# The second half of a decoder's key tiles in products of 256 columns, and its activations 96 bytes further on

## The chip, the core and the metric

The kernel runs on one core of one Trainium2 chip, one program launched once. The time is the device time in microseconds (us), the median of the runs of a kernel. Engines are called as in the profile: PE is the matrix engine TensorE and PEld its weight loads, ACT is ScalarE, DVE is VectorE, POOL is GpSimd, SP issues the loads from memory.

## The reference

One block of a decoder over 256 tokens of width 1024: first a mixer of a convolution branch and a dilated attention branch, then a retrieval from 16384 experts. The retrieval is what the change touches:

```
q = (xc @ w_q).reshape(TOKEN_CHUNK, PEER_HEADS, 2, half)
s = jnp.einsum('thpd,hpnd->thpn', q, sub_keys)
top_s, top_i = lax.top_k(s, PEER_TOPK)
...
e = i1 * PEER_N_KEYS + i2
gate = jax.nn.softmax(best_s, axis=-1)
h = jnp.einsum('thkd,td->thk', u_tab[e], xc)
act = jax.nn.gelu(h, approximate=False) * gate
return jnp.einsum('thk,thkd->td', act, v_tab[e])
```

## The kernel before

The kernel does not gather experts. It computes the product of every expert row of `u_tab` with every token, takes the gelu, multiplies by a gate that is zero for experts a token has not picked, and multiplies the result by all of `v_tab`. Each table is read as 128 tiles of 128 x 1024 numbers. The program has a front part (76 weight tiles and the attention), then 128 key tiles (U) and then 128 value tiles (V).

**Precision.** Every tile comes in float32 into `raw`. ACT rounds it into `hi` (line 335) and DVE or POOL writes the rest `raw - hi` into `lo` (line 354). The other operand is split the same way: the normed tokens into `nrm_hi` and `nrm_lo`, the activations into `act_hi` and `act_lo`. A product of two numbers is then hi times hi, hi times lo and lo times hi.

**Key tiles 0 to 63** run in `u_tile`: per tile 8 blocks of 128 numbers, and per block three products of 256 columns into one bank: 24 products a tile (line 1242, in `product`). `hi` or `lo` is the operand that PE loads as weights (stationary), the tokens stream through (moving). ACT then takes the gelu out of the bank (line 645).

**Key tiles 64 to 127** run in `wide_tile`. `nrm_hi` and `nrm_lo` of a block lie side by side, so `hi` meets both in one product of 512 columns (line 1499), whose right half goes into the right half of the bank; `lo` meets `nrm_hi` in one of 256 (line 1501). That is 16 products a tile. The two halves of the bank have to be added: ACT copies the right one into `half_sum` (line 666), DVE adds the left one (line 1167), and ACT takes the gelu of the sum (line 671). PE may write a bank again when `added` says that the tile two before has been summed.

**The gates.** Beside these tiles run 32 groups of small products (line 1513, 16 to a group, 128 x 64 in float16) that spread the gates of 8 tokens over the experts of the first half. DVE makes their operands and multiplies the gates into `act`. The first two groups stand ahead of tiles 64 and 66, the others in pairs ahead of every fourth tile. PE thus starts a row of large products 17 times. Another 32 groups stand among the first 64 value tiles in the same way.

**Value tiles** run in `v_tile`: 12 products of 512 columns each (line 1564, the last two tiles in line 1590), and here `act_hi` and `act_lo` are the weights and `hi` and `lo` stream. The activations lie in the space of the tokens, which are no longer needed: the two views of `norm_space` are

```
norm_space = sb("norm_space", [P, KB * 2 * T + SHIFT], F32R)
nrm = norm_space[:, SHIFT:].rearrange("p (k a t) -> p k a t", a=2, t=T)
picked_acts = norm_space[:, 0:RING * 2 * T].rearrange("p (k a t) -> p k a t", a=2, t=T)
```

Every slice that PE loads or streams starts at a multiple of 512 bytes from the start of its view. So all slices of a view have one place modulo 512. Counted from the start of `norm_space`, the tokens are at place 32, the activations at 0, and `hi` and `lo` at 96. `rounded_space`, which holds the streamed operand in parts of the front, is placed at 32 as well.

**The order of the work** is written out by hand, with semaphores between engines. `raw`, `hi` and `lo` have 4 slots each; SP loads a tile into a slot when its `lo` is done.

Of the kernel before, what the change touches and what calls it, by code (L numbers as in the profile page):

```python
# [11 lines left out]
ALU = mybir.AluOpType  # L12
ACT = mybir.ActivationFunctionType
AX = mybir.AxisListType

P = 128
D = 1024
T = 256
KB = D // P
# [23 lines left out]
RING = 4  # L43
LEAD = 3
AHEAD = 2

SHIFT = 8
CHUNK_STEPS = PH // 2 + 9
TOP_TILES = 48
EXP_TILE = 52  # L50
PICK_TILE = 60
HALF = NK // 2
# [112 lines left out]
def hybrid_block(nc, x_t, front, cols, rel_bias, onehot, sub_keys, u_tiles, v_tiles, out):  # L165
    bias_row = nc.dram_tensor("bias_row", (HEADS, BW), F32, kind="Internal").ap()
    toeplitz = nc.dram_tensor("toeplitz", (HEADS, P * BW), F32, kind="Internal").ap()
    with ExitStack() as ctx:
        def sb(name, shape, dt=F32, stack=ctx):
            return stack.enter_context(nc.sbuf_tensor(name, shape, dt))  # L170

        def sem(name):
            return ctx.enter_context(nc.semaphore(name))

        bank = [ctx.enter_context(nc.psum_tensor(f"bank{i}", [P, 512], F32)) for i in range(8)]


        norm_space = sb("norm_space", [P, KB * 2 * T + SHIFT], F32R)
        nrm = norm_space[:, SHIFT:].rearrange("p (k a t) -> p k a t", a=2, t=T)
        nrm_hi, nrm_lo = nrm[:, :, 0, :], nrm[:, :, 1, :]  # L180
        picked_acts = norm_space[:, 0:RING * 2 * T].rearrange("p (k a t) -> p k a t", a=2, t=T)
        act_hi, act_lo = picked_acts[:, :, 0, :], picked_acts[:, :, 1, :]
        ident = sb("ident", [P, P])
        iota = sb("iota", [P, TOPK])
# [35 lines left out]
        act = sb("act", [P, NK, T])  # L220
# [3 lines left out]
        parts = sb("parts", [P, T // PAIR, 2, PAIR], F16)  # L224
        ohA = sb("ohA", [P, 2, TOK // PAIR, NK, PAIR], F16)
        eqB = sb("eqB", [P, TOK // PAIR, HALF, PAIR], F16)
        half_sum = sb("half_sum", [P, 2, T])
        ohB = sb("ohB", [P, 2, TOK // PAIR, 2, HALF, PAIR], F16)
        raw = sb("raw", [P, RING, D])
        hi = sb("hi", [P, RING, D], F32R)  # L230
        lo = sb("lo", [P, RING, D], F32R)
# [42 lines left out]
        pe_step = sem("pe_step")  # L274
# [15 lines left out]
        attn_gated, merged, m_hi = sem("attn_gated"), sem("merged"), sem("m_hi")  # L290
        chain = sem("chain")
        sc_ready = sem("sc_ready")
        crossed, added, gelu_done = sem("crossed"), sem("added"), sem("gelu_done")
        top_done, gexp, gate_ready, pick_T, pick_ready = [sem(s) for s in (
            "top_done", "gexp", "gate_ready", "pick_T", "pick_ready")]
        second, spread, gate_mm, gated = sem("second"), sem("spread"), sem("gate_mm"), sem("gated")
        blocks_free = sem("blocks_free")
# [31 lines left out]
        def split_hi(act_e, base, it, j):  # L329

            s = slot_of(base, j)
            wait_raw(act_e, base, it, j)
            if not (isinstance(it, int) and base + 4 * it + j < RING):
                wait(act_e, pe_step, step_of(base - 4, it, j))
            act_e.copy(hi[:, s, :], raw[:, s, :]).then_inc(hi_ready, 1)  # L335
# [11 lines left out]
        def wait_lo(eng, base, it, j):  # L347
            eng.wait_ge(lo_ready[slot_of(base, j)], uses(base, it, j))
# [116 lines left out]
        def _(a):  # L465
# [193 lines left out]
                    gelu(0, it, j)  # L659

            a.wait_ge(pick_ready, 2)
            def copy_cross(it, j):

                a.wait_ge(pe_step, it * 4 + (S_U + HALF + j + 1))
                a.wait_ge(gelu_done, it * 4 + (HALF + j - 1))
                a.copy(half_sum[:, j % 2, :], bank[4 + j % 2][:, T:2 * T]).then_inc(crossed, 1)  # L666

            def gelu_sum(base, it, j):

                a.wait_ge(added, it * 4 + (base + j + 1))  # L670
                a.activation(act[:, it * 4 + (HALF + base + j), :], half_sum[:, (base + j) % 2, :], ACT.Gelu)\
                 .then_inc(gelu_done, 1)

            def a_split(base_i, it, j):

                wait(a, pe_step, it * 4 + (S_V + base_i + j - 3))
                a.copy(act_hi[:, (base_i + j) % RING, :], act[:, it * 4 + (base_i + j), :]).then_inc(a_hi, 1)  # L677

            def key_round(it, first=False, last=False):
                for j in range(RING):  # L680
                    if last and j == RING - 1:
                        a.wait_ge(gated, GROUPS_N)
                        a.wait_ge(blocks_free, 1)
                        for first_act in range(AHEAD):
                            a_split(first_act, 0, 0)
                    copy_cross(it, j)
                    if not (first and j == 0):
                        gelu_sum(-1, it, j)
                    split_hi(a, U0 + HALF + LEAD, it, j)

            key_round(0, first=True)
            with a.Fori(1, HALF // RING - 1) as it:
                key_round(it)
            key_round(HALF // RING - 1, last=True)
            gelu_sum(HALF - 1, 0, 0)

            a.wait_ge(pe_step, S_V)
            for half in range(2):
# [19 lines left out]
        def _(dve):  # L718
# [438 lines left out]
            def low_part(base_i, it, j):  # L1157

                dve.wait_ge(a_hi, it * 4 + (base_i + j + 1))
                s = (base_i + j) % RING  # L1160
                dve.tensor_tensor(act_lo[:, s, :], act[:, it * 4 + (base_i + j), :], act_hi[:, s, :].bitcast(F32),  # L1161
                                  ALU.subtract).then_inc(a_lo, 1)

            def add_halves(it, j):

                dve.wait_ge(crossed, it * 4 + (j + 1))
                dve.tensor_tensor(half_sum[:, j % 2, :], bank[4 + j % 2][:, 0:T], half_sum[:, j % 2, :], ALU.add)\
                   .then_inc(added, 1)

            def gate_body(half, it, first=False, last=False):  # L1170

                base = U0 + HALF if half == 0 else V0
                for j in range(RING):
                    if j == 0 and first:

                        dve.wait_ge(gelu_done, HALF * (half + 1))
                    if half == 1 and not (last and j >= RING - AHEAD):
                        low_part(AHEAD, it, j)
                    if first and j % 2 == 0:
                        multiply(half, it, j // 2)  # L1180
                    elif j == 0:
                        multiply(half, it, 0)
                        multiply(half, it, 1)
                    if first and j in (1, 2):
                        one_hots(half, it, 1 + j)
                    elif not first and j in (1, 2) and not last:
                        one_hots(half, it, 1 + j)
                    elif j in (1, 2) and last and half == 0:
                        one_hots(1, 0, j - 1)
                    if half == 0:  # L1190
                        if last and j == RING - 1:
                            for first_act in range(AHEAD):
                                low_part(first_act, 0, 0)
                        add_halves(it, j)
                    if by_dve(base + LEAD, j):
                        split_lo(dve, base + LEAD, it, j)

# [24 lines left out]
        def _(pe):  # L1222
# [13 lines left out]
            def product(dst, s, units, vec_hi, vec_lo, base, it, j, first=True, last=True):  # L1236

                wait_lo(pe, base, it, j)
                n = len(units)
                for i, (u, k) in enumerate(units):  # L1240
                    for p_, (w_, x_) in enumerate(((hi, vec_hi), (hi, vec_lo), (lo, vec_hi))):
                        ins = pe.matmul(dst, w_[:, s, u * P:(u + 1) * P], x_[:, k, :],  # L1242
                                        start=first and i == 0 and p_ == 0, stop=last and i == n - 1 and p_ == 2)
                return ins
# [207 lines left out]
            b = start(("ssq2",))  # L1452
# [27 lines left out]
                if BANK_OF[job] < 6:  # L1480
                    freed(pe, job)

            def u_tile(base_i, it, j):

                wait(pe, gelu_done, it * 4 + (base_i + j - 1))
                ins = product(bank[4 + j % 2][:, 0:T], j, [(k, k) for k in range(KB)], nrm_hi, nrm_lo, U0 + base_i, it, j)
                ins.then_inc(pe_step, 1)

            def wide_tile(it, j, last=False):

                b = bank[4 + j % 2]
                if isinstance(it, int) and it == 0 and j < 2:
                    pe.wait_ge(gelu_done, HALF + j - 1)
                else:
                    pe.wait_ge(added, it * 4 + (j - 1))
                wait_lo(pe, U0 + HALF, it, j)
                for k in range(KB):
                    unit = slice(k * P, (k + 1) * P)
                    pe.matmul(b[:, :], hi[:, j, unit], nrm[:, k, :, :].rearrange("p a t -> p (a t)"),  # L1499
                              start=k == 0, stop=False, skip_group_check=True)  # L1500
                    ins = pe.matmul(b[:, 0:T], lo[:, j, unit], nrm_hi[:, k, :],  # L1501
                                    start=False, stop=k == KB - 1, skip_group_check=True)
                    if last and k == RING - 1:
                        ins.then_inc(blocks_free, 1)
                ins.then_inc(pe_step, 1)

            def gates(half, it, g):
# [35 lines left out]
            def u_and_gates(it, last=False):  # L1543
                for j in range(RING):
                    for g in groups_ahead(it, j):
                        gates(0, it, g)
                    wide_tile(it, j, last and j == RING - 1)

            u_and_gates(0)
            with pe.Fori(1, HALF // RING - 1) as it:  # L1550
# [114 lines left out]
```

## Time and profile before

| | us |
|---|---|
| median of 3 runs (1012.19 to 1013.17) | 1012.79 |
| the profiled execution | 1012.39 |
| its span, first to last instruction | 1010.6 |
| PE busy | 1006.0 |
| DVE busy | 794.4 |
| ACT busy | 526.2 |
| POOL busy | 460.8 |

A product's own duration in the profile (some 280 ns for 256 columns) holds the way through the array, on which the next product follows closely, so the durations overlap. What a product costs is the distance from its start to the start of the next one. It is read from the starts in the timeline, or from a row of the chain, which gives the time and the number of a run of products.

### The profile page before, as it was taken

How to read it: one execution, taken by the hardware profiler on the slowest of the kernel's cores; microseconds unless marked ns; L12 is line 12 of the kernel's file. 1: busy time of each engine (PE TensorE's matmuls, PEld its weight loads, DVE VectorE, ACT ScalarE, POOL GpSimd, SP SyncE). 2: the span in 40 equal slices, each digit the busy share in tenths (PEclk: the TensorE clock that was granted, in tenths of full speed). 3: DMA queues.
4: the chain of work that ended last, by engine and by line, in shares of the span. 5: the costliest groups of instructions: out<-in, count | busy, mean ns of one | idle time of the engine just before them, and what ended most of it. 6: DMA issues, size and time to landing. Idle time of an engine off the chain costs nothing.

```text
span 1010.6 us, 21094 instructions
## 1 busy us (share of the span) xinstructions
PE 1006.0 (100%) x7310; PEld 898.7 (89%) x7310; DVE 794.4 (79%) x1368; ACT 526.2 (52%) x853; POOL 460.8 (46%) x198
## 2 busy tenths in 40 slices
PE   9999999999999999999999999999999999999998
PEld 9999999999999999988888888788888888888886
DVE  6999785867999993288888888988888867676764
ACT  6654877644545445545555555544444444444443
POOL 4654456756699999943444433100000004444442
DMA  6684446655455566545554455555555555655562
GB/s 240 225 290 157 132 147 201 200 183 167 149 187 193 181 205 201 192 153 170 175 172 166 166 166 168 192 184 176 174 166 166 170 183 173 201 176 197 177 198 83
DMA packets 52618, 181.93 MB, mean 180 GB/s; under 512 B 5943, under 2 KB 9155, under 8 KB 52452
## 3 DMA queue, kind: packets, MB, share of 16 engines
q1 hardware_dynamic: 52292, 181.16, 54.2%
q8 instruction: 24, 0.39, 0.2%
q10 hardware_dynamic: 288, 0.27, 0.1%
q14 instruction: 14, 0.11, 0.0%
HBM read 180.33 MB, written 3.43 MB: 182 GB/s over the span
## 4 chain that ended last, share of the span: by engine, by line
PE 97%; ACT 1%; DVE 1%; issue 0%; POOL 0%; DVEq 0%; ACTq 0%; POOLq 0%
PE bank L1564 35%; PE bank L1242 33%; PE bank L1499 12%; PE bank L1501 6%; PE bank L1513 3%; PE bank L1343 2%; PE bank L1257 1%; PE bank L1475 1%; PE bank L1590 1%; PE bank L1266 1%; ACT hi L335 1%; PE bank L1359 1%; PE bank L1382 0%; DVE lo L354 0%; PE bank L1370 0%
## 5 line engine op out<-in xcount | busy, mean ns | idle before, releaser
L354 POOL TENSOR_TENSOR lo<-raw,hi 128x1024 fp32r<-128x1024 f32 x184 | 457.9, 2503 | 535.3 <-ACT hi L335 535.0
L335 ACT CAST hi<-raw 128x1024 fp32r<-128x1024 f32 x332 | 347.3, 1047 | 224.0 <-PE bank L1564 193.5
L1564 PE MATMUL bank<-hi,norm_space 128*128 128x512 f32 x1008 | 280.3, 397 | 0.0
L1242 PE MATMUL bank<-norm_space,hi 128*128 128x256 f32 x1600 | 276.4, 278 | 0.2 <-POOL lo L354 0.2
L1242 PEld LDWEIGHTS bank<-norm_space,hi 128*128 128x128 f32 x1600 | 241.6, 188 | 1.8 <-issue 1.2
L1564 PEld LDWEIGHTS bank<-hi,norm_space 128*128 128x128 f32 x1008 | 187.9, 188 | 44.6
L354 DVE TENSOR_TENSOR lo<-raw,hi 128x1024 fp32r<-128x1024 f32 x148 | 189.4, 1280 | 44.3 <-ACT hi L335 41.7
L1242 PE MATMUL bank<-norm_space,lo 128*128 128x256 f32 x800 | 221.6, 277 | 0.0
L1499 PE MATMUL bank<-norm_space,hi 128*128 128x512 f32 x512 | 182.8, 400 | 0.0
L1564 PE MATMUL bank<-lo,norm_space 128*128 128x512 f32 x504 | 158.3, 395 | 0.0
L1161 DVE TENSOR_TENSOR norm_space<-act,norm_space 128x256 fp32r<-128x256 f32 x128 | 111.2, 871 | 50.3 <-ACT norm_space L677 50.3
L1242 PEld LDWEIGHTS bank<-norm_space,lo 128*128 128x128 f32 x800 | 150.3, 188 | 0.0
L1501 PE MATMUL bank<-norm_space,lo 128*128 128x256 f32 x512 | 143.8, 281 | 0.0
L1499 PEld LDWEIGHTS bank<-norm_space,hi 128*128 128x128 f32 x512 | 96.3, 188 | 22.8
L1564 PEld LDWEIGHTS bank<-lo,norm_space 128*128 128x128 f32 x504 | 94.6, 188 | 22.8
L1501 PEld LDWEIGHTS bank<-norm_space,lo 128*128 128x128 f32 x512 | 96.2, 188 | 0.0
L1242 PE MATMUL bank<-rounded_space,hi 128*128 128x256 f32 x496 | 87.0, 280 | 0.0
L1242 PEld LDWEIGHTS bank<-rounded_space,hi 128*128 128x128 f32 x496 | 75.3, 188 | 0.9 <-issue 0.6
L666 ACT COPY half_sum<-bank 128x256 f32<-128x256 f32 x64 | 23.9, 374 | 92.1 <-PE bank L1501 92.1
L1242 PE MATMUL bank<-rounded_space,lo 128*128 128x256 f32 x248 | 69.1, 278 | 0.0
L645 ACT ACTIVATE act<-bank 128x256 f32 x64 | 24.6, 384 | 83.7 <-PE bank L1242 83.7
L1136 DVE TENSOR_TENSOR eqB<-iota_nk,keys 128x512 f16<-128x512 f16 x64 | 60.5, 945 | 0.1
(190 smaller groups left out, 955.4 us busy)
## 6 DMA issues: line engine op xcount, KB each, us to landing
raw<-u_tiles SPq DMA_DIRECT2D x128, 512.0 KB, 3.3
raw<-v_tiles SPq DMA_DIRECT2D x128, 512.0 KB, 3.3
raw<-front SPq DMA_DIRECT2D x76, 512.0 KB, 4.0
toeplitz<-bias_row SPq DMA_DIRECT2D x6, 384.0 KB, 7.4
bias<-toeplitz SPq DMA_DIRECT2D x12, 128.0 KB, 4.0
resid<-x_t SPq DMA_DIRECT2D x2, 512.0 KB, 4.6
qk<-sub_keys SPq DMA_DIRECT2D x1, 1024.0 KB, 7.7
y<-act SPq DMA_DIRECT2D x3, 256.0 KB, 2.0
```

Of the source, the lines that this page charges most:

```text
L335: act_e.copy(hi[:, s, :], raw[:, s, :]).then_inc(hi_ready, 1)
L354: eng.tensor_tensor(lo[:, s, :], raw[:, s, :], hi[:, s, :].bitcast(F32), ALU.subtract)\
L645: a.activation(act[:, it * 4 + (base_i + j), :], bank[4 + j % 2][:, 0:T], ACT.Gelu).then_inc(gelu_done, 1)
L666: a.copy(half_sum[:, j % 2, :], bank[4 + j % 2][:, T:2 * T]).then_inc(crossed, 1)
L1136: dve.tensor_tensor(eqB[:, :, :, :], every_pair(iota_nk[:, half * HALF:(half + 1) * HALF, :], HALF), at(keys[:, 1, t], HALF), ALU.is_equal ...
L1161: dve.tensor_tensor(act_lo[:, s, :], act[:, it * 4 + (base_i + j), :], act_hi[:, s, :].bitcast(F32), ALU.subtract).then_inc(a_lo, 1)
L1242: ins = pe.matmul(dst, w_[:, s, u * P:(u + 1) * P], x_[:, k, :], start=first and i == 0 and p_ == 0, stop=last and i == n - 1 and p_ == 2)
L1343: ins = pe.matmul(b[:, c * T:(c + 1) * T], x_[:, k, c * P:(c + 1) * P], w_[:, n % RING, 2 * m * P:2 * (m + 1) * P], start=k == 0 and c == ...
L1499: pe.matmul(b[:, :], hi[:, j, unit], nrm[:, k, :, :].rearrange("p a t -> p (a t)"), start=k == 0, stop=False, skip_group_check=True)
L1501: ins = pe.matmul(b[:, 0:T], lo[:, j, unit], nrm_hi[:, k, :], start=False, stop=k == KB - 1, skip_group_check=True)
L1513: ins = pe.matmul(bank[6 + g][:, q * HALF:(q + 1) * HALF], ohA[:, g, q // PAIR, :, q % PAIR], ohB[:, g, q // PAIR, i, :, q % PAIR], start= ...
L1564: ins = pe.matmul(bank[2 * c + half][:, :], a_[:, j, c * P:(c + 1) * P], v_[:, j, half * 512:(half + 1) * 512], start=False, stop=False, s ...
```

## The change

The last 64 key tiles go back to `u_tile` with its 24 products of 256 columns, and the copy, the sum and their buffer go. ACT takes the gelu directly out of the bank. The wait on `added` becomes the wait on `gelu_done` that the first 64 tiles have. The last of these tiles is issued as two calls of `product`, 4 blocks and 4 blocks, so that `blocks_free` still tells ACT and DVE after the fourth block that the tokens' first four blocks may be overwritten. The view of the activations starts 24 numbers (96 bytes) further on, so at place 96, that of `hi` and `lo`.

```
+ACT_SHIFT = 24
...
-        picked_acts = norm_space[:, 0:RING * 2 * T].rearrange("p (k a t) -> p k a t", a=2, t=T)
+        picked_acts = norm_space[:, ACT_SHIFT:ACT_SHIFT + RING * 2 * T].rearrange("p (k a t) -> p k a t", a=2, t=T)
...
-        half_sum = sb("half_sum", [P, 2, T])
...
-            def key_round(it, first=False, last=False):
+            def key_round(it, last=False):
                 for j in range(RING):
+                    split_hi(a, U0 + HALF + LEAD, it, j)
                     if last and j == RING - 1:
...
-                    copy_cross(it, j)
-                    if not (first and j == 0):
-                        gelu_sum(-1, it, j)
-                    split_hi(a, U0 + HALF + LEAD, it, j)
...
+                    gelu(HALF, it, j)
...
-                        add_halves(it, j)
...
-            def u_tile(base_i, it, j):
+            def u_tile(base_i, it, j, last=False):
 
                 wait(pe, gelu_done, it * 4 + (base_i + j - 1))
...
+                b, units = bank[4 + j % 2][:, 0:T], [(k, k) for k in range(KB)]
+                if last:
+                    product(b, j, units[:RING], nrm_hi, nrm_lo, U0 + base_i, it, j, last=False).then_inc(blocks_free, 1)
+                    ins = product(b, j, units[RING:], nrm_hi, nrm_lo, U0 + base_i, it, j, first=False)
                 else:
...
-                for k in range(KB):
-                    unit = slice(k * P, (k + 1) * P)
-                    pe.matmul(b[:, :], hi[:, j, unit], nrm[:, k, :, :].rearrange("p a t -> p (a t)"),
-                              start=k == 0, stop=False, skip_group_check=True)
-                    ins = pe.matmul(b[:, 0:T], lo[:, j, unit], nrm_hi[:, k, :],
-                                    start=False, stop=k == KB - 1, skip_group_check=True)
...
-                    wide_tile(it, j, last and j == RING - 1)
+                    u_tile(HALF, it, j, last and j == RING - 1)
```

PE, in the loop over the second half of the key tiles, before: two groups of gates, then the first blocks of a tile.

```order
L1513 MATMUL bank<-ohB,ohA 128x64 x16
L1510 ISA
L1513 MATMUL bank<-ohB,ohA 128x64 x16
L1495 ISA
L348 REGISTER_ALU
L1499 MATMUL bank<-norm_space,hi 128x512
L1501 MATMUL bank<-norm_space,lo 128x256
```

The same place after the change; the large products are now those of line 1218, which was line 1242.

```order
L1476 MATMUL bank<-ohB,ohA 128x64 x16
L1473 ISA
L1476 MATMUL bank<-ohB,ohA 128x64 x16
L304 ISA
L348 REGISTER_ALU
L1218 MATMUL bank<-norm_space,hi 128x256 x2
L1218 MATMUL bank<-norm_space,lo 128x256
```

One product of 512 columns has become two of 256 behind the same groups of gates; nothing else stands between them.

ACT, in the same loop, before: the work for one tile.

```order
L666 COPY half_sum<-bank 128x256
L671 ISA
L671 ACTIVATE act<-half_sum 128x256
L327 ISA
L304 REGISTER_ALU
L335 CAST hi<-raw 128x1024
```

ACT after the change, the work for one tile.

```order
L335 CAST hi<-raw 128x1024
L644 REGISTER_ALU
L645 ISA
L645 ACTIVATE act<-bank 128x256
```

The copy is gone, and the rounding of a later tile now stands ahead of the gelu.

DVE, in the same loop, two neighbouring places before.

```order
L1142 TENSOR_TENSOR ohB<-eqB,parts 128x1024
L1166 REGISTER_ALU
L1167 TENSOR_TENSOR half_sum<-bank,half_sum 128x256
L353 REGISTER_ALU
L354 TENSOR_TENSOR lo<-raw,hi 128x1024
```

And after.

```order
L1126 TENSOR_TENSOR ohB<-eqB,parts 128x1024
L353 REGISTER_ALU
L354 TENSOR_TENSOR lo<-raw,hi 128x1024
```

The sum has gone from ahead of the split, and with it its wait on ACT's copy.

## Rows read from the trace of the kernel before

**Rows 1.** The page: busy time of each engine, and the chain by engine.

```profile
PE 1006.0 (100%) x7310; PEld 898.7 (89%) x7310; DVE 794.4 (79%) x1368; ACT 526.2 (52%) x853; POOL 460.8 (46%) x198
...
PE 97%; ACT 1%; DVE 1%; issue 0%; POOL 0%; DVEq 0%; ACTq 0%; POOLq 0%
```

**Rows 2.** The stretch of tiles 64 to 127: busy times, granted clock, DMA.

```profile
core 0: us, PE busy (x) PEld busy (x) DVE busy (x) ACT busy (x) POOL busy (x), PEclk, DMA share, GB/s
434.02:631.76 197.74, 197.74 (x1538) 172.22 (x1537) 163.86 (x223) 104.88 (x191) 76.56 (x32) 1.00 0.51 167
```

**Rows 3.** The chain in order of time: start us, us, what.

```profile
152.73 57.34 PE bank L1242 x504
...
215.44 36.75 PE bank L1242 x312
...
259.33 163.29 PE bank L1242 x1440
...
817.03 184.89 PE bank L1564 x792
```

**Rows 4.** PE's timeline in tiles 64 to 127, behind a pair of gate groups.

```profile
start us, us, engine line op out<-in xcount [idle before <-releaser]
...
472.15 0.48 PE L1499 MATMUL bank<-norm_space,hi 128*128 128x512 f32 x1
472.46 0.28 PE L1501 MATMUL bank<-norm_space,lo 128*128 128x256 f32 x1
...
472.92 0.40 PE L1499 MATMUL bank<-norm_space,hi 128*128 128x512 f32 x1
...
475.75 0.40 PE L1499 MATMUL bank<-norm_space,hi 128*128 128x512 f32 x1
```

**Rows 5.** The gate products in that stretch: their busy time and number.

```profile
434.02:631.76 197.74, 18.43 (x512) 16.39 (x513) 1.00 0.51 167
```

**Rows 6.** The gates' first group: its start, and the start of what follows.

```profile
434.02 0.66 PE L1513 MATMUL bank<-ohB,ohA 128*128 128x64 f16 x16
434.51 0.48 PE L1499 MATMUL bank<-norm_space,hi 128*128 128x512 f32 x1
```

**Rows 7.** Restarts of rows of 256 columns, at 423 and at 215 us.

```profile
423.04 0.49 PE L1242 MATMUL bank<-norm_space,hi 128*128 128x256 f32 x2
423.36 0.28 PE L1242 MATMUL bank<-norm_space,lo 128*128 128x256 f32 x1
423.48 0.39 PE L1242 MATMUL bank<-norm_space,hi 128*128 128x256 f32 x2
...
215.19 0.48 PE L1242 MATMUL bank<-rounded_space,hi 128*128 128x256 f32 x2
215.51 0.28 PE L1242 MATMUL bank<-rounded_space,lo 128*128 128x256 f32 x1
```

**Rows 8.** Groups of ACT and DVE instructions that go or change, mean ns after the comma.

```profile
L666 ACT COPY half_sum<-bank 128x256 f32<-128x256 f32 x64 | 23.9, 374 | 92.1 <-PE bank L1501 92.1
L671 ACT ACTIVATE act<-half_sum 128x256 f32 x56 | 23.5, 421 | 0.7
L1167 DVE TENSOR_TENSOR half_sum<-bank,half_sum 128x256 f32<-128x256 f32 x64 | 26.7, 417 | 20.9 <-ACT half_sum L666 20.9
```

**Rows 9.** ACT's timeline in the first half of the key tiles.

```profile
300.36 0.38 ACT L645 ACTIVATE act<-bank 128x256 f32 x1 [1.40 <-PE bank L1242]
300.64 1.05 ACT L335 CAST hi<-raw 128x1024 fp32r<-128x1024 f32 x1
303.08 0.38 ACT L645 ACTIVATE act<-bank 128x256 f32 x1 [1.39 <-PE bank L1242]
```

**Rows 10.** The waits from 434 to 633 us: who for whom, us in total, times, longest.

```profile
POOL lo L354 <- ACT hi L335: 119.8, 31, 6.3
ACT half_sum L666 <- PE bank L1501: 92.1, 64, 3.0
DVE half_sum L1167 <- ACT half_sum L666: 20.9, 16, 2.0
```

More of the change, by code:

```diff
@@ L292, in hybrid_block @@
         sc_ready = sem("sc_ready")
-        crossed, added, gelu_done = sem("crossed"), sem("added"), sem("gelu_done")
+        gelu_done = sem("gelu_done")
         top_done, gexp, gate_ready, pick_T, pick_ready = [sem(s) for s in (
@@ L661, in _ @@
             a.wait_ge(pick_ready, 2)
[L662 to L672, printed above, removed]
             def a_split(base_i, it, j):
@@ L685, in key_round @@
                             a_split(first_act, 0, 0)
-                    copy_cross(it, j)
-                    if not (first and j == 0):
-                        gelu_sum(-1, it, j)
-                    split_hi(a, U0 + HALF + LEAD, it, j)
-            key_round(0, first=True)
-            with a.Fori(1, HALF // RING - 1) as it:
+                    gelu(HALF, it, j)
+            with a.Fori(0, HALF // RING - 1) as it:
                 key_round(it)
             key_round(HALF // RING - 1, last=True)
-            gelu_sum(HALF - 1, 0, 0)
             a.wait_ge(pe_step, S_V)
@@ L1162, in low_part @@
                                   ALU.subtract).then_inc(a_lo, 1)
[L1164 to L1168, printed above, removed]
             def gate_body(half, it, first=False, last=False):
@@ L1189, in gate_body @@
                         one_hots(1, 0, j - 1)
[L1190 to L1193, printed above, removed]
-                        add_halves(it, j)
+                    if half == 0 and last and j == RING - 1:
+                        for first_act in range(AHEAD):
+                            low_part(first_act, 0, 0)
                     if by_dve(base + LEAD, j):
@@ L1481, in _ @@
                     freed(pe, job)
-            def u_tile(base_i, it, j):
+            def u_tile(base_i, it, j, last=False):
                 wait(pe, gelu_done, it * 4 + (base_i + j - 1))
[L1486 to L1493, printed above, removed]
-                else:
-                    pe.wait_ge(added, it * 4 + (j - 1))
-                wait_lo(pe, U0 + HALF, it, j)
-                for k in range(KB):
-                    unit = slice(k * P, (k + 1) * P)
-                    pe.matmul(b[:, :], hi[:, j, unit], nrm[:, k, :, :].rearrange("p a t -> p (a t)"),
-                              start=k == 0, stop=False, skip_group_check=True)
-                    ins = pe.matmul(b[:, 0:T], lo[:, j, unit], nrm_hi[:, k, :],
-                                    start=False, stop=k == KB - 1, skip_group_check=True)
-                    if last and k == RING - 1:
-                        ins.then_inc(blocks_free, 1)
+                b, units = bank[4 + j % 2][:, 0:T], [(k, k) for k in range(KB)]
+                if last:
+                    product(b, j, units[:RING], nrm_hi, nrm_lo, U0 + base_i, it, j, last=False).then_inc(blocks_free, 1)
+                    ins = product(b, j, units[RING:], nrm_hi, nrm_lo, U0 + base_i, it, j, first=False)
+                else:
+                    ins = product(b, j, units, nrm_hi, nrm_lo, U0 + base_i, it, j)
                 ins.then_inc(pe_step, 1)
```

## The prediction

> **What bounds the kernel now.** The page first: PE is busy for the whole span and the chain lies on it for 97% [rows 1]. So nothing counts but how fast PE starts one product after the other, and whether the change makes it wait. The stretch of the changed tiles, 434.02 to 631.76 us, has PE busy in all of its 197.74 us at full clock (1.00, the 2.4 GHz level), while DVE is at 164 us, ACT at 105 and POOL at 77; the DMA engines are at half their share [rows 2]. The removed work of ACT and DVE is therefore off the path, and what the change gives or takes is PE's own beat.
>
> Next I read that beat from the chain, which gives the time and number of a run of products. In key tiles 0 to 59 it is 163.29 us for 1440 products, 113.4 ns each. But the same products have a second beat: 36.75 us for 312, 117.8 ns each, in a late part of the front, and 57.34 us for 504, 113.8 ns, in an earlier one [rows 3]. The slices' places modulo 512 are the same in all three, PE has no gap, and in each case the beat is held over many tiles. The reader is to see two things: there is a fast and a slow beat for 256 columns, 4% apart, and whatever sets it is decided where a row of products starts anew, since it then stays. Now the wide tiles: from 472.92 to 475.75 us are 8 blocks, 354 ns for each pair of 512 and 256 columns [rows 4]. Three products at the slow beat are 3 x 117.8 = 353.4 ns. So per column the wide tiles run at the slow beat, and three fast products would take 340.2 ns. The value tiles: 184.89 us for 792 products of 512 columns, 233.4 ns each [rows 3], which is between twice the fast beat (226.8) and twice the slow one (235.6).
>
> **The products of the second half.** First the sum for the stretch as it is. A group of 16 gate products takes 434.51 - 434.02 = 0.49 us [rows 6], and there are 512 products, 32 groups [rows 5]: 15.7 us. A wide row starts 17 times; its first two pairs take 472.92 - 472.15 = 0.77 us against 2 x 0.354, so 0.06 us extra each [rows 4], 1.0 us in all. The remaining 197.74 - 15.7 - 1.0 = 181.0 us over 512 blocks are 353.6 ns a block, which agrees with the pair read directly.
>
> After the change there are 64 x 24 = 1536 products of 256 columns, the same 32 groups and the same 17 restarts. A restart of such products is seen in both beats. At 423.04 us the first three products take 0.44 us and the row goes on fast: 0.44 - 3 x 0.1134 = 0.10 us extra. At 215.19 the first two take 0.32 us and the row goes on slow: 0.32 - 2 x 0.1178 = 0.08 us extra [rows 7].
> At the fast beat: 1536 x 0.1134 = 174.2, + 15.7 + 17 x 0.10 = 191.6 us, against 197.7: 6.1 us less.
> At the slow beat: 1536 x 0.1178 = 180.9, + 15.7 + 17 x 0.08 = 198.0 us: 0.3 us more.
> These are the two ends for this part; no row shows products of 256 columns behind a float16 group. I take the fast one: it holds for the 1440 products of the first half, whose tiles, places, banks and waits are those that the second half gets. The loop also repeats one restart 15 times, so I expect one beat for nearly all rounds, not a mixture.
>
> **The work that goes.** ACT loses a copy of 374 ns a tile and its gelu of 421 ns becomes one like that of the first half, 0.38 us; DVE loses 417 ns a tile [rows 8, 9]. I cost both at nothing. The cover is PE: ACT waited 92.1 us for it here and POOL 119.8 us for ACT [rows 10]. Without that cover the copy would be worth 24 us and the sum 27 us. Where does the stall go? PE now waits for the gelu of the tile two before. In the first half ACT has 0.38 + 1.05 us of work in a tile and then 1.4 us of idle time until PE ends the next one [rows 9]; the gelu is done within 1.05 + 0.38 us of the tile's end even when a rounding stands ahead of it, and PE needs it after a whole tile, 24 x 113.4 ns = 2.7 us. So there is no new wait. Queued behind a waiting gelu is the rounding three tiles ahead, and behind that the splits of POOL and DVE; the loads follow those. With 1.3 us to spare none of them comes late. DVE's 20.9 us of waits on ACT's copy [rows 10] go too, so its splits come earlier, and the loads with them; at a DMA share of 0.51 they meet nothing new.
>
> **The seam to the value tiles.** ACT and DVE prepare the first two activations when four blocks of the last tile are through, as before. The last gelu no longer has a copy and a sum ahead of it. PE had no idle time there and has none to gain: 0.
>
> **The place of the activations.** In the value tiles the weights move from place 0 to 96, where the streamed slices lie. No row has such a pair with 512 columns, so this is bounded from both sides. There are 1536 products of 512 columns. Down: twice the fast beat, 226.8 ns, gives (226.8 - 233.4) x 1.536 = -10.1 us. Up: the step between the two beats, 117.8 / 113.4 = 1.039, on top of 233.4 gives 242.5 ns and +14.0 us. Nearest by far is the beat as it is, since the rows of the key tiles, with the streamed slices at 32 and the weights at 96, show beats within 3% of it per column. I take 0, and keep -10.1 and +14.0. A gain is likelier than a loss: 233.4 is already close to the slow beat per column, so there is more known ground below than above.
>
> The sum against the profiled execution's own 1012.39 us: 1012.39 - 6.1 = 1006.3. The median of the runs is 0.4 us above it: 1006.7 us.
>
> **Two rules of the Trainium skill that speak against this change.** What the rows show is above: 113.4 or 117.8 ns for 256 columns and 233.4 for 512 [rows 3]. The Trainium skill, "TensorE: Matmul & The Clock Gate", section "Back-to-back issue gap", gives columns / 2.4 + 2.5 ns for an isolated one. By it (an estimate from that page) a block is 215.8 + 109.2 = 325.0 ns wide and 3 x 109.2 = 327.5 ns narrow, so the change would cost 512 x 2.5 ns = 1.3 us. The trace doesn't agree with the figures: the wide block takes 354 ns. The same page, Part 2, says that PE reads the streamed operand and the weights through two independent ports of SBUF, by which the new place of the activations changes nothing; no run here shows it yet.
>
> **The rivals.**
> 1. *The value tiles gain as well.* The moved weights bring the 512-column products to twice the fast beat: -10.1 us more, 996.6 us; with the key tiles left at the slow beat 1012.79 + 0.3 - 10.1 = 1003.0. For it: 233.4 is no multiple of either beat of 256 columns, so something between the two operands slows these products that need not. Against it: nothing in the trace ties a beat to a place.
> 2. *The change doesn't do what it says.* Each row behind a float16 group falls into the slow beat, as the wide ones do in every round [rows 4], and the place is indifferent: +0.3 us, 1013.1 us, no change. For it: of the runs of products in rows 3 one is slow, and wide tiles behind these groups are all slow. Against it: the fast beat of the first half.
> 3. *The value tiles lose.* The streamed slice and the weight slice now start at the same place, and if PE's two reads get in each other's way there, each product of lines 1564 and 1590 gets longer. At 242.5 ns it is +14.0 - 6.1 = +7.9 us, 1020.7 us. It decides from +4.0 ns a product (6.1 us / 1536), that is from 237.4 ns. For it: nothing is known of the pair. Against it: PE reads 4 bytes a column in either place.
> 4. *ACT becomes the bound.* If the gelu came later than 2.7 us after its tile, PE would stop once a tile. Rows 9 leave 1.3 us, so I give this no chance of its own.
>
> **How the numbers follow.** Likeliest: fast beat in the key tiles, value tiles within 1 ns of before, 1006.7 us (1005 to 1009 alone): 0.36. Rival 1: 0.33, of which 0.10 with slow key tiles. Rival 2: 0.18. Rival 3: 0.13, a third of it so small that the sum stays near the time before or below it. A measurement of this kernel can tell about 0.2% (2 us) from no change. Faster: 0.36 + 0.33 + 0.02 = 0.71. The same: 0.17 of rival 2 and 0.01 of rival 3. Slower: 0.11. The range reaches from just under the time of both gains to a small loss: 995 to 1015 us. It leaves out a loss in the value tiles near its bound, and a gain beyond twice the fast beat.
>
> **What the profile after would show.** Key tiles 64 to 127: the chain's runs of 96 products between pairs of gate groups, 10.9 us each if fast and 11.3 if slow; the stretch 191.6 or 198.0 us long. Value tiles: the chain's run of 792 products, 184.9 us if the place is indifferent, 179.6 if it is twice the fast beat, above 188.0 if rival 3 decides. PE without idle time throughout. ACT idle some 1.2 us or more before each gelu. The prediction is wrong if the runs of 96 are slow, if the run of 792 moves by over 1 us, or if a wait of PE on a gelu shows.

## The result, and the profile after

The changed kernel takes 997.07 us, the median of 3 runs (996.33 to 997.09), against 1012.79. The ratio is 0.9845 with a 95% interval of 0.9825 to 0.9864: 15.7 us less, faster by 1.55%. The forecast was 1006.7 us, and 996.6 us for its rival 1.

The stretch of key tiles 64 to 127 in the profile after, the columns as in [rows 2]:

```profile
core 0: us, PE busy (x) PEld busy (x) DVE busy (x) ACT busy (x) POOL busy (x), PEclk, DMA share, GB/s
434.35:626.19 191.84, 191.84 (x2055) 191.22 (x2054) 146.58 (x163) 87.10 (x130) 82.90 (x33) 1.00 0.53 177
```

It is 191.84 us instead of 197.74, 5.9 us less. The chain of the changed kernel shows the beat (start us, us, what):

```profile
259.66 163.29 PE bank L1218 x1440
...
435.00 5.54 PE bank L1218 x48
...
441.05 5.73 PE bank L1218 x48
...
459.73 10.97 PE bank L1218 x96
...
483.65 10.97 PE bank L1218 x96
...
626.68 5.56 PE bank L1527 x24
...
807.08 179.64 PE bank L1527 x792
```

The first half of the key tiles is the same to 0.01 us as in [rows 3]. A round of the second half takes 10.97 us for 96 products, restart included; 96 x 113.4 ns are 10.89, so it is the fast beat. The 17 rows that the gate groups cut are these rounds of 96 products, 15 of them, and two of 48 ahead of them. One of the 17 is slow: the row that starts at 441.05 us with 5.73 us for 48 products, where the one before it took 5.54.

The value tiles have moved as well: 179.64 us for 792 products, 226.8 ns each, where [rows 3] had 184.89 us and 233.4 ns. The value tiles of the kernel before start here:

```profile
632.42 5.68 PE bank L1564 x24
```

So the value tiles ahead of that run took 817.03 - 632.42 = 184.6 us before and 807.08 - 626.68 = 180.4 us after, 4.2 us less. With 5.9 us from the key tiles, 5.25 us from the run of 792 and 0.2 us in the last two tiles that makes 15.5 us; the span became 15.4 us shorter.

Nothing new waits. The waits of the changed kernel from 434 to 627 us (who for whom, us in total, times, longest):

```profile
POOL lo L354 <- ACT hi L335: 108.9, 32, 4.1
ACT act L645 <- PE bank L1218: 105.5, 65, 2.4
DVE act L1138 <- PE bank L1476: 41.6, 15, 2.9
```

These are engines that wait for PE or for what PE has freed. ACT is idle 1.6 us a tile before its gelu (105.5 / 65), so the cover was there. PE has no wait in this stretch and none in the value tiles.

### The profile page after: what moved, and what is told of

Same layout as the page of the kernel before. It is cut to its first block, busy times and chain, and to the rows that moved or that the text cites. A ratio compares the mean times of both kernels' runs of the same rounds, so it can differ in the third digit from the quotient of the medians.

```text
span 995.2 us, 21854 instructions
## 1 busy us (share of the span) xinstructions
PE 989.8 (99%) x7822; PEld 917.0 (92%) x7822; DVE 774.9 (78%) x1304; ACT 506.8 (51%) x789; POOL 465.3 (47%) x198
## 4 chain that ended last, share of the span: by engine, by line
PE 93%; DVE 5%; ACT 1%; issue 0%; POOL 0%; ACTq 0%; DVEq 0%; POOLq 0%
PE bank L1218 50%; PE bank L1527 35%; DVE bank L798 3%; PE bank L1476 3%; PE bank L1319 1%; PE bank L1233 1%; PE bank L1451 1%; DVE lo L354 1%; PE bank L1242 1%; PE bank L1553 1%; PE bank L1335 1%; ACT hi L335 0%; PE bank L1358 0%; PE bank L1346 0%; PE bank L1249 0%
## 5 line engine op out<-in xcount | busy, mean ns | idle before, releaser
L1218 PE MATMUL bank<-norm_space,hi 128*128 128x256 f32 x2624 | 452.4, 278 | 0.2 <-POOL lo L354 0.2
L1218 PEld LDWEIGHTS bank<-norm_space,hi 128*128 128x128 f32 x2624 | 396.2, 188 | 1.8 <-issue 1.2
L1527 PE MATMUL bank<-hi,norm_space 128*128 128x512 f32 x1008 | 273.8, 391 | 0.0
L645 ACT ACTIVATE act<-bank 128x256 f32 (+1 forms) x128 | 49.2, 384 | 187.8 <-PE bank L1218 187.8
L1138 DVE SCALAR_TENSOR_TENSOR act<-bank,act 128x512 f32 (+1 forms) x64 | 41.4, 686 | 51.7 <-PE bank L1476 51.7
L1126 DVE TENSOR_TENSOR ohB<-eqB,parts 128x1024 f16<-128x1024 f16 x64 | 81.4, 1272 | 0.0
L665 ACT CAST norm_space<-act 128x256 fp32r (+1 forms) x128 | 51.4, 402 | 0.1
L1218 PEld LDWEIGHTS bank<-rounded_space,lo 128*128 128x128 f32 x248 | 47.0, 190 | 0.0
L798 DVE SCALAR_TENSOR_TENSOR bank<-u_pad,prm,bank 128x256 f32<-128x256 f32 x116 | 46.3, 481 | 0.0
L1122 DVE TENSOR_TENSOR ohA<-iota_nk,keys 128x1024 f16<-128x1024 f16 x64 | 46.1, 720 | 0.0
```

The source lines that it names most:

```text
L645: a.activation(act[:, it * 4 + (base_i + j), :], bank[4 + j % 2][:, 0:T], ACT.Gelu).then_inc(gelu_done, 1)
L798: dve.scalar_tensor_tensor(out=acc[:, b, :] if w == TAPS - 1 else part_sum, in0=src, scalar=wt, in1=part_sum, op0=ALU.mult, op1=ALU.add).t ...
L1122: dve.tensor_tensor(ohA[:, g % 2], every_pair(iota_nk[:, :, :], NK), at(keys[:, 0, t], NK), ALU.is_equal).then_inc(spread, 1)
L1126: dve.tensor_tensor(ohB[:, g % 2].rearrange("p a i n b -> p (a i) n b"), eqB[:, :, :, :].unsqueeze(2).broadcast_to([P, TOK // PAIR, 2, HAL ...
L1138: dve.scalar_tensor_tensor(out=av, in0=gv, scalar=1.0 / GATE_SCALE, in1=av, op0=ALU.mult, op1=ALU.mult)\
L1527: ins = pe.matmul(bank[2 * c + half][:, :], a_[:, j, c * P:(c + 1) * P], v_[:, j, half * 512:(half + 1) * 512], start=False, stop=False, s ...
```

## The experiments

All runs are compared with the kernel before on the same chip, whose median was 1012.2 to 1012.8 us in every set. A time without a range is that of one run; the beats are from its profile. "Distance" below is the start of the weights' slices minus the start of the streamed slices, in bytes.

**1. The two halves of the change apart.** The changed kernel with its activations back at place 0:

```
-ACT_SHIFT = 24
+ACT_SHIFT = 0
```

> The changed kernel with the activations back at place 0 of norm_space; the key tiles stay in products of 256 columns. Place theory (the value tiles' beat follows from where the weights lie modulo 512): the run of 792 value products goes back to 233.4 ns each, the kernel to 996.7 + 10 = about 1007 us. Rival, freed buffer (without half_sum, hi and lo lie 2048 bytes lower, and that made the value tiles fast): they stay at 226.8 ns, 997 us. Both expect the 96-product runs of the key tiles at 10.98 us.

Measured: 1006.68 us (1005.97 to 1007.07), ratio 0.9938 (0.9921 to 0.9954). Its chain:

```profile
811.21 184.89 PE bank L1527 x792
```

The value tiles are back at 233.4 ns, though `hi` and `lo` still lie 2048 bytes lower. The freed buffer is not the cause. And 1006.68 us is what the prediction gave for key tiles at the fast beat and value tiles as before, to 0.1 us.

The kernel before with only the activations moved:

```
-        picked_acts = norm_space[:, 0:RING * 2 * T].rearrange("p (k a t) -> p k a t", a=2, t=T)
+        picked_acts = norm_space[:, 24:24 + RING * 2 * T].rearrange("p (k a t) -> p k a t", a=2, t=T)
```

> The kernel before with its wide key tiles and half sums; only the activations lie 24 numbers further on. Place theory: value products 226.8 ns, 1012.8 - 10.1 = 1002.7 us, key tiles unchanged at 353.6 ns a block. Freed buffer theory: value products stay at 233.4 ns, 1012.8 us.

Measured: 1002.53 us (1002.38 to 1002.95), ratio 0.9897 (0.9881 to 0.9914). The chain, and the stretch of the wide key tiles:

```profile
813.01 179.64 PE bank L1564 x792
```

```profile
434.30:632.00 197.70, 197.70 (x1538) 172.18 (x1537) 163.80 (x223) 104.89 (x191) 76.50 (x32) 1.00 0.52 168
```

The key tiles did not move (197.70 against 197.74 us), the value tiles did. The place is worth 1012.8 - 1002.5 = 10.3 us and the narrow products 1012.8 - 1006.7 = 6.1 us; together 16.4, and both in one kernel gave 15.7 in its own set. The 0.7 us between these sums is within the spread of the sets (0.6 to 1.6 us from the lowest to the highest time of one kernel). In the traces the parts add up: the run of 792 takes 179.64 us with wide key tiles as with narrow ones, and the narrow key tiles with their gates take 626.07 - 434.39 = 191.68 us with the activations at 0, by the chain

```profile
434.39 0.50 PE bank L1476 x16
...
626.07 0.50 PE bank L1476 x16
```

and the same 191.68 us in the changed kernel (434.51 to 626.19 in its chain). Neither part disturbs the other.

**2. Which place.** The change is named after equal places modulo 512. Six runs of the changed kernel have only the activations at other places, with `ACT_SHIFT` of 8, 16, 28, 56, 88 and 152 numbers; for the last three `norm_space` is 512 bytes longer, so that all other buffers keep their place modulo 512:

```
-        norm_space = sb("norm_space", [P, KB * 2 * T + SHIFT], F32R)
+        norm_space = sb("norm_space", [P, KB * 2 * T + 8 + 128], F32R)
```

> The changed kernel with the activations at place 32 instead of 96 (so 64 bytes below hi and lo modulo 512, the same place modulo 64). If only equal places modulo 512 are fast: about 233 ns a value product, +10 us against the changed kernel, 1007 us. Rival, modulo 64 (the weights' slice must lie at the same place within 64 bytes): 226.8 ns, 997 us.

> The changed kernel with the activations 512 bytes further on still (place 608, which is 96 modulo 512); norm_space is 512 bytes longer, so all later buffers keep their place modulo 512. Equal place modulo 512: 226.8 ns a value product, 997 us. Rival, the absolute address of the activations or their distance from hi counts: another beat, 233 ns and 1007 us.

> The changed kernel with the activations at place 352, 256 bytes away from hi and lo modulo 512. Measured so far are 233.3 ns a value product at 96 bytes below, 228.9 at 64 below and 226.7 at equal places. Place modulo 512: a slow beat, 233 ns or more, 1007 us. Rival, a period of 256 bytes or less: 226.7 ns, 997 us.

> The changed kernel with the activations at place 64, 32 bytes below hi and lo. If the beat grows steadily with the distance: between 226.7 and 228.9 ns, about 998 us. If 226.7 is a floor that the nearest places share: 226.7 ns, 997 us. If what counts is place 32 modulo 64, which places 32 and 96 share: about 233 ns, 1007 us.

> The changed kernel with the activations at place 224, 128 bytes past hi and lo. So far the value products took 226.7 ns at distances of 0, 256 and 512 bytes, 228.9 at 64, and 233.3 at 32 and 96. If the period is 128 bytes: 226.7 ns, 997 us. If it is 256 bytes: another beat, 228.9 ns or more, 1000 us or more. Modulo 512, the rule that the change is named after, is refuted by the run at 256 already, unless 256 is a second fast place.

> The changed kernel with the activations at place 112, 16 bytes past hi and lo. If the fast places are wide (some tens of bytes): 226.7 ns a value product, 997 us. If the distance has to be 0 modulo the period: 228.9 to 233.3 ns, 1000 to 1007 us.

The run of 792 value products in each:

| kernel | distance | 792 products, us | each, ns | time, us |
|---|---|---|---|---|
| before; activations at 0 | -96 | 184.89 | 233.4 | 1012.79; 1006.68 |
| activations at 32 | -64 | 181.38 | 229.0 | 1000.62 |
| at 64 | -32 | 184.88 | 233.4 | 1007.14 |
| the change | 0 | 179.64 | 226.8 | 997.07 |
| 16 bytes further | +16 | 184.87 | 233.4 | 1007.23 |
| 128 further | +128 | 184.12 | 232.5 | 1005.19 |
| 256 further | +256 | 179.64 | 226.8 | 996.61 |
| 512 further | +512 | 179.64 | 226.8 | 996.94 |

The fast places are narrow: 16 bytes aside is as slow as 96. They come again after 256 bytes, but not after 128. So equal places modulo 512, the rule that the change is named after, ask for more than is needed: 256 bytes off is as fast. A steady growth with the distance is refuted too, since 32 bytes are slower than 64.

**3. Place or distance.** Here everything but the activations lies 32 bytes further on (`norm_space` 544 bytes longer, the tokens at 16 numbers instead of 8), and then the activations too.

> The changed kernel with hi, lo, raw, the tokens and rounded_space all 32 bytes further on; only the activations stay where they are, now 32 bytes below hi and lo. If the distance between weights and streamed slices counts: 233.4 ns a value product, 1007 us. Rival, the activations' own place modulo 256 counts, whatever streams: 226.8 ns, 997 us. Key tiles keep their distance of 64 bytes and their runs of 10.98 us in the first case.

> The same with the activations moved along, so that every place is 32 bytes further on and every distance as in the changed kernel. Distance: 226.8 ns and 997 us. Own place: 233 ns, 1007 us.

Measured: 1005.75 us and 997.13 us. The chains of the first and of the second:

```profile
810.39 184.88 PE bank L1527 x792
```

```profile
807.19 179.64 PE bank L1527 x792
```

The activations at an unmoved place are slow when the values move away by 32 bytes, and fast again when they follow. It is the distance between the two operands.

A rival is left: other engines and the DMA also read and write these buffers, and what they meet there moves with the places. The traces of before and after settle it. Each has a stretch near its end in which DVE, ACT and POOL do nothing and no DMA runs (columns as in [rows 2]):

```profile
999.10:1003.30 4.20, 4.20 (x20) 3.38 (x19) 0.00 (x0) 0.00 (x0) 0.00 (x0) 1.00 0.00 0
```

```profile
984.10:988.10 4.00, 4.00 (x19) 3.34 (x18) 0.00 (x0) 0.00 (x0) 0.00 (x0) 1.00 0.00 0
```

PE's timeline at its two ends, before and then after, with 17 products from the first start to the second:

```profile
999.42 0.63 PE L1564 MATMUL bank<-lo,norm_space 128*128 128x512 f32 x2
...
1003.39 0.39 PE L1590 MATMUL bank<-lo,norm_space 128*128 128x512 f32 x1
```

```profile
984.29 0.62 PE L1527 MATMUL bank<-lo,norm_space 128*128 128x512 f32 x2
...
988.14 0.39 PE L1553 MATMUL bank<-lo,norm_space 128*128 128x512 f32 x1
```

That is 3.97 / 17 = 233.5 ns and 3.85 / 17 = 226.5 ns: both beats stay with PE alone at work.

**4. The same distance for products of 256 columns.** The kernel before with the tokens at place 96 (`norm_space` is again 512 bytes longer; `rounded_space` stays at 32):

```
-        nrm = norm_space[:, SHIFT:].rearrange("p (k a t) -> p k a t", a=2, t=T)
+        nrm = norm_space[:, 24:24 + KB * 2 * T].rearrange("p (k a t) -> p k a t", a=2, t=T)
```

> The kernel before, wide key tiles and half sums, with the tokens at place 96 instead of 32, so the streamed slices start where hi and lo do; activations at 0 as before. If the wide tiles' slow beat comes from the place: 340 ns a block instead of 353.6, 1012.8 - 7 = 1006 us. Rival, it comes from the width (512 and 256 columns in turn): 353.6 ns a block, 1013 us. The value tiles stay at 233.3 ns in both.

Measured: 1023.86 us (1023.31 to 1024.53), ratio 1.0115 (1.0098 to 1.0132). It was slower where I expected a gain. First the chain's run in the first half of the key tiles, then PE's timeline in the second:

```profile
263.70 172.85 PE bank L1242 x1440
```

```profile
501.89 0.39 PE L1499 MATMUL bank<-norm_space,hi 128*128 128x512 f32 x1
...
504.66 0.39 PE L1499 MATMUL bank<-norm_space,hi 128*128 128x512 f32 x1
```

The wide blocks did get faster: (504.66 - 501.89) / 8 = 346 ns instead of 353.6, though not 340. One product of 512 columns at 226.8 ns and one of 256 at 120.0, which are the beats that each width has at distance 0, would be 346.8. But the narrow products of the first half went from 113.4 to 172.85 / 1440 = 120.0 ns, 9.6 us in this run alone, which my expectation had left out.

The changed kernel with tokens and `rounded_space` at place 96 too:

> The changed kernel with the tokens and rounded_space at place 96 too, so that every streamed slice and every weight slice starts at the same place modulo 512. If equal places always give the fast beat, also behind a restart: the slow runs of the front (312 products at 117.8 ns, 192 more at 35 us and others, some 850 products in all) gain 4.4 ns each, about 3.8 us, 993.3 us. Rival, the two beats of 256 columns have nothing to do with the place: 997 us.

Measured: 1023.33 us (1022.92 to 1023.59), ratio 1.011 (1.0093 to 1.0127).

```profile
266.08 172.85 PE bank L1218 x1440
...
640.65 11.59 PE bank L1218 x96
```

All runs of narrow products in the key tiles are now at 120 ns or a little more, and none is fast. The theory that equal places are good for all products is refuted. Four further distances, with tokens and `rounded_space` together:

> The changed kernel with the tokens and rounded_space at place 64, 32 bytes below hi and lo. Products of 256 columns had two beats (113.3 and 117.8 ns) at place 32 and one of 120.0 at place 96. If the beat of narrow products gets worse towards equal places: between these, 118 ns, some 1010 us or more. If a distance of 32 bytes lets them always run fast: 113.3 ns everywhere, 3 to 4 us less in the front, 993.5 us.

> The same with the tokens and rounded_space at place 0, 96 bytes below hi and lo (32 bytes from them modulo 128). If a period of 128 bytes holds for narrow products, and the side does not matter: the same beat as with the tokens at 64. Otherwise a beat of its own: 113.3 ns everywhere would be 993.5 us, 117.8 about 1009 us.

> The changed kernel with the tokens and rounded_space at place 224, 128 bytes past hi and lo. The value tiles keep 226.8 ns. Products of 256 columns so far: two beats (113.4 and 117.8 ns) at 64 bytes below, 118.4 at 32 below, 117.4 at 96 below, 120.0 at equal places. If the two beats follow from the distance, this one has its own: 113.3 ns everywhere would take 3 to 4 us from the front and the restarts, 993.5 us; 117 ns or more everywhere would be 1012 us or more. If it is like equal places with a period of 128 bytes: 120 ns, 1023 us.

> The changed kernel with the tokens and rounded_space at place 160, 64 bytes past hi and lo. If the side does not matter: the same two beats as at 64 bytes below, 997 us within 1 us. If it does and the fast beat is always reached: 993.5 us; if never: 1012 us or more.

| kernel | distance | 1440 products of the first half, us | each, ns | time, us |
|---|---|---|---|---|
| the change | 64 | 163.29 | 113.4 | 997.07 |
| tokens at 0 | 96 | 169.03 | 117.4 | 1014.57 |
| tokens at 64 | 32 | 170.46 | 118.4 | 1015.45 (1015.04 to 1016.38) |
| tokens at 96 | 0 | 172.85 | 120.0 | 1023.33 |
| tokens 64 past | -64 | 163.27 | 113.4 | 1006.09 (1005.68 to 1006.59) |
| tokens 128 past | -128 | 170.95 | 118.7 | 1020.07 (1019.96 to 1020.75) |

The column "each" is the beat of that one run. With the tokens 128 past, the first half ran at 118.7 ns, but in the second half only the first round of 96 products took 11.47 us and the other 14 took 11.59 or 11.60 us, as long as a round at distance 0:

```profile
265.01 170.95 PE bank L1218 x1440
...
461.61 11.47 PE bank L1218 x96
...
474.07 11.60 PE bank L1218 x96
...
637.61 11.59 PE bank L1218 x96
```

So 64 bytes is not the only distance with more than one beat. But only 64 bytes, on either side, reached the fast one. There the beat of a row changes only where the row starts anew. That is best seen with the tokens 64 past: the first half of its key tiles runs fast, but all 15 rounds of 96 products of its second half are slow, each with 11.38 or 11.39 us:

```profile
261.84 163.27 PE bank L1218 x1440
...
598.91 11.39 PE bank L1218 x96
...
623.64 11.39 PE bank L1218 x96
```

The changed kernel's rounds take 10.97 us, at the same width and, but for the side, the same distance. The difference is 15 x 0.41 = 6.2 us of the 9 us that this kernel is slower; the run of 504 products in the front, 59.55 us instead of 57.34, is another 2.2. What picks the beat at a restart stays open. The distance alone does not: the changed kernel's first row of 48 took 5.54 us, and the same row took 5.73 us with the activations at 32, whose key tiles are the same in code and places:

```profile
435.38 5.73 PE bank L1218 x48
...
441.61 5.73 PE bank L1218 x48
```

No place was found at which the slow beat never comes, and none of these kernels beats the change.

**5. Width or operands.** The changed kernel with its value tiles in products of 256 columns:

```
-                            for half in range(2):
-                                ins = pe.matmul(bank[2 * c + half][:, :], a_[:, j, c * P:(c + 1) * P],
-                                                v_[:, j, half * 512:(half + 1) * 512],
+                            for q in range(4):
+                                ins = pe.matmul(bank[2 * c + q // 2][:, q % 2 * T:(q % 2 + 1) * T], a_[:, j, c * P:(c + 1) * P],
+                                                v_[:, j, q * T:(q + 1) * T],
```

> The changed kernel with the value tiles in products of 256 columns, 24 a tile, at equal places (all but the last two tiles). If equal places are bad for narrow products whatever the operands are: 120.0 ns each, as the tokens at place 96 gave, 997 + 20 = 1017 us. Rival, it is the key tiles' operands that make equal places bad: 113.3 ns, 997 us.

Measured: 1015.87 us.

```profile
802.81 11.59 PE bank L1527 x96
...
815.38 190.15 PE bank L1527 x1584
```

The long run takes 190.15 / 1584 = 120.0 ns a product, and a round of 96 takes 11.59 us: the value tiles now have the very beat of the key tiles at equal places. So it is the width that decides there, and not which operands they are. At a distance of 0 two products of 256 columns cost 240 ns, one of 512 costs 226.8.

## Why the prediction was wrong

- **The sum of the key tiles was right.** It said 191.6 us at the fast beat, the stretch took 191.84; it said -6.1 us, the narrow products alone gave -6.1 us. One restart of 17 fell into the slow beat and cost 5.73 - 5.54 = 0.2 us. The choice between the beats was a guess from the first half of the tiles, and that it held was partly luck: the kernel with the tokens 64 past shows that it can go the other way in just this loop, which was rival 2's mechanism and worth 6.4 us. Nor is it shown that the wide tiles ran "at the slow beat": 353.6 ns was close to 3 x 117.8, but at distance 0 a block took what its two widths take there, 346 ns, and not three equal beats.
- **The removed work and the seam cost nothing**, as said: no wait of PE, and ACT idle 1.6 us a tile.
- **The step that failed is "I take 0, and keep -10.1 and +14.0"** for the place of the activations. In its place the runs showed -10.3 us (the place alone), the lower bound to 0.2 us: 226.8 ns a product, twice the fast beat. That the bound was met so closely is luck in part: it came from products of 256 columns at a distance of 64, and at the distance of 0 that the change sets, these take 120.0 ns. No run shows why 226.8 is twice 113.4. The argument for 0 was that "the rows of the key tiles, with the streamed slices at 32 and the weights at 96, show beats within 3% of it per column". That compared different widths, and closeness of beats is no evidence that a place is indifferent: 3% of 348 us is 10 us. The prediction's "against" for rival 1, that nothing in the trace ties a beat to a place, was true, and only meant that the trace could not decide.
- **Rival 1 came true in full**, with a chance of 0.23 in its full form, and 996.6 us as its time. Its ground, that 233.4 is a multiple of neither beat, was the part of the profile that pointed the right way. It pointed at a gain to be had, not at the place that gives it: 229.0 and 232.5 ns at other places are no multiples either.
- **Rival 3** did not come here, but what it feared is real for the other width: with equal starts products of 256 columns took 120.0 instead of 113.4 ns, 6.6 ns longer.
- **The rules of the Trainium skill.** Per-product cost (the Trainium skill, "TensorE: Matmul & The Clock Gate", "Back-to-back issue gap"): by it the narrow products would have cost 1.3 us (an estimate from that page), they gave 6.1. By the two independent read ports of the same page of the Trainium skill, Part 2, all rows of the first table of experiment 2 would be alike. They run from 226.8 to 233.4 ns, so PE's two operands can't be placed without regard to each other. Other engines and the DMA are ruled out by the stretches with PE alone. Whether it is PE's two reads that meet was not shown: no run took the weight loads away.

## What to carry to other kernels

When PE is busy throughout, read the distance from start to start of its products, and compare it per column between stages: a stage that is slower per column than another at the same clock has something to gain, even where no engine waits. For products of fp32r operands try the distance between the weights' and the streamed slices, for each width by itself: first 0, then steps of 32 bytes from there, as 16 bytes aside already lost all. Here 0, 256 and 512 bytes were best for 512 columns, and 0 was the worst of the six distances tried for 256. A term for which no row exists should get its chances from its bounds and not a 0 because the present value lies near; if it is worth 1% either way, the forecast should say that it hangs on it.

## What the runs showed of the hardware

- A product of 512 columns in fp32r took 226.8 ns (distances 0, 256 and 512), 229.0 (-64), 232.5 (128) or 233.4 (-96, -32 and 16), with only the activations moved between these kernels; 16 bytes made 6.6 ns. With everything moved by the same 32 bytes it stayed at 226.8, and with DVE, ACT, POOL and DMA idle both 226.5 and 233.5 ns are seen.
- Products of 256 columns took 120.0 ns at a distance of 0, in the key tiles and in the value tiles. In the first half of the key tiles they took 118.4 at 32, 117.4 at 96 and 118.7 at -128, where most later rounds were as slow as at 0. At 64 bytes, on either side, they have two lasting beats, 113.4 and 117.8 ns, and change between them only at a restart. What picks one isn't shown.
- The granted clock was 1.00 in every profile (no run below 0.999), at the fast beats and at the slow ones, so the beats are no matter of the clock.
